# Turning back the second S5 half on GpSimd, with the S5 output products inside the inverse, in a two-layer hybrid decoder trunk

## The reference, cut to what matters

```
bu = einsum(u, b_bar);  states = scan: s[t] = lam_bar * s[t-1] + bu[t]      (complex, 1024 states)
y  = einsum(c_mat, states).real + d_skip * u;  y = gelu(y);  y = y * sigmoid(y @ glu_w + glu_b)
p  = softmax(q k^T / 8, causal);  y_moba = p @ v
g  = -exp(a_log) * softplus(a + dt_bias);  beta = sigmoid(b)
chunks of 64 tokens: (I + strictly_lower(beta k k^T * decay))^-1 applied to v and k, then a scan over 4 chunks
```

## Time and profile before

| | before |
|---|---|
| median of 3 runs | 1687.88 us (1685.31 to 1690.2) |
| the profiled execution, its own time | 1689.82 us |
| its span, first to last instruction | 1688.0 us |
| mean granted TensorE clock | 0.966 |
| TensorE busy | 1571.5 us, 93% of the span |
| VectorE busy | 1273.0 us, 75% |
| ScalarE busy | 920.9 us, 55% |
| GpSimd busy | 162.8 us, 10% |

### The profile page before, as it was taken

The page is one execution under the profiler, slowest core; times in us unless marked ns, Lnnn a source line. Parts: engine busy times, 40 slices in busy tenths (PEclk is TensorE's granted clock), DMA queues, the critical chain, the costliest instruction groups (busy, mean ns, idle before and its releaser), DMA issues.

```text
span 1688.0 us, 22489 instructions
## 1 busy us (share of the span) xinstructions
PE 1571.5 (93%) x8642; PEld 1267.0 (75%) x8642; DVE 1273.0 (75%) x1136; ACT 920.9 (55%) x761; POOL 162.8 (10%) x177
## 2 busy tenths in 40 slices
PE   8888999999898797599999999999999999999991
PEld 7657478888776574488888888888888888888881
DVE  7985655444529756388888888888888888888883
ACT  1144133434204331377777777777777777777770
POOL 0342085000004400200000000000000000000000
PEclk9989999999999998799999999999999999999996
DMA  8693165554433202699999999999999999999962
GB/s 311 247 314 137 52 218 205 198 176 152 171 133 118 76 3 100 237 363 374 355 395 391 355 394 370 375 395 348 398 394 349 395 395 350 396 389 366 393 254 89
DMA packets 192882, 469.57 MB, mean 278 GB/s; under 512 B 7024, under 2 KB 11248, under 8 KB 192304
## 3 DMA queue, kind: packets, MB, share of 16 engines
q1 hardware_dynamic: 189360, 453.70, 73.3%
q0 software_dynamic: 2304, 10.77, 1.6%
q10 hardware_dynamic: 1152, 4.19, 0.6%
HBM read 461.29 MB, written 25.17 MB: 288 GB/s over the span
## 4 chain that ended last, share of the span: by engine, by line
issue 59%; PE 28%; DVE 10%; DMA 1%; ACT 1%; POOL 1%; POOLq 0%; SPq 0%; DVEq 0%
PE ps L1429 9%; PE ps L1402 4%; PE ps L1440 4%; PE ps L1755 2%; DVE arena L960 2%; PE ps L1409 1%; PE ps L1693 1%; DVE arena L993 1%; PE ps L1707 1%; PE ps L1703 1%; DVE arena L977 1%; DVE small L1013 1%; DMA arena<-in_w_in 0%; DVE x L1021 0%; DVE x L1025 0%
## 5 line engine op out<-in xcount | busy, mean ns | idle before, releaser
L1036 DVE TENSOR_TENSOR lo<-arena,hi 128x2048 fp32r<-128x2048 f32 x378 | 868.4, 2302 | 222.5 <-ACT hi L641 221.9
L641 ACT ACTIVATE hi<-arena 128x2048 fp32r<-128x2048 f32 x378 | 723.3, 1919 | 356.8 <-PE ps L1429 229.8
L1429 PE MATMUL ps<-hi,xg 128*128 128x512 f32 x1792 | 556.0, 392 | 3.2 <-DVE xg L1042 2.6
L1429 PEld LDWEIGHTS ps<-hi,xg 128*128 128x128 f32 x1792 | 336.7, 189 | 75.9 <-DVE lo L1036 3.4
L1429 PE MATMUL ps<-lo,xg 128*128 128x512 f32 x896 | 350.1, 391 | 0.0
L1440 PE MATMUL ps<-hi,hTe 128*128 128x512 f32 x896 | 283.8, 398 | 2.2 <-DVE hTe L1066 2.2
L1429 PEld LDWEIGHTS ps<-lo,xg 128*128 128x128 f32 x896 | 169.0, 189 | 35.5
L1440 PEld LDWEIGHTS ps<-hi,hTe 128*128 128x128 f32 x896 | 164.8, 189 | 35.0 <-DVE lo L1036 2.6
L1440 PE MATMUL ps<-lo,hTe 128*128 128x512 f32 x448 | 175.8, 392 | 0.0
L1429 PE MATMUL ps<-hi,xs 128*128 128x512 f32 x448 | 140.1, 394 | 2.9 <-issue 2.9
L1402 PE MATMUL ps<-arena 128*128 128x256 f32 x544 | 126.2, 395 | 3.4 <-DMA arena<-in_w_in 2.2
(11 more groups left out here) (329 smaller groups left out, 1371.5 us busy)
## 6 DMA issues: line engine op xcount, KB each, us to landing
arena<-in_mg SPq DMA_DIRECT2D x112, 1024.0 KB, 7.0
arena<-in_mu SPq DMA_DIRECT2D x112, 1024.0 KB, 6.9
arena<-in_md SPq DMA_DIRECT2D x112, 1024.0 KB, 7.0
arena<-in_w_in SPq DMA_DIRECT2D x7, 2048.0 KB, 11.2
arena<-in_wg SPq DMA_DIRECT2D x14, 1024.0 KB, 5.1
arena<-in_wu SPq DMA_DIRECT2D x14, 1024.0 KB, 5.1
arena<-in_wd SPq DMA_DIRECT2D x14, 1024.0 KB, 4.9
xg_rows<-in_zeros SPq DMA_DIRECT2D x1, 8704.0 KB, 35.2
```

The lines of the kernel that those rows point to most:

```text
L641: af(hi[r % PARTS][:, :], raw[r % RAWS], ACT.Copy).then_inc(hi_ready, 1)
L1036: tt(lo[r % PARTS][:, :], raw[r % RAWS], hi[r % PARTS][:, :].bitcast(F32), ALU.subtract)\
L1429: ins = mm(ps[:, (4 if w == "G" else 4 + nb) + b, :], tok[a][:, kk * nt + b * P:kk * nt + (b + 1) * P], tiles_of(part[r % PARTS], w)[:, k, ...
```

## The change

Six edits:

1. `turn_forward(..., 1)` leaves VectorE. GpSimd runs it behind its whole convolution, once `turned_back` reaches its second count, and signals `states_ready`.
2. On VectorE, `convolve(l, 4)` now stands ahead of `s5_rotate(l, 1)`.
3. The norm of the probabilities moves behind the gates (behind the two `beta` operations).
4. TensorE's S5 output products move from ahead of L1626 to round `v == 2` of the inverse, behind its X and Y products, and write bank 7. VectorE's skip term moves to round `v == 3`, behind `kd` and the clearing of `S`.
5. The buffers move: `pT` to the start of `phase` (the cosine table), `M[0]` into the convolution's input, `uT`, `dt_`, `Tm`, `M[1]` and `tg` elsewhere.
6. New waits follow from that: ScalarE waits for `states_ready` before its first copy to `pT`, VectorE for `conv_v` before its first `M[0]`. TensorE no longer waits for `y_sum` between the transposes.

```diff
-O_PT = 8448
-O_LA, O_U, O_DT, O_T, O_A, O_MM = 0, 1536, 2304, 3072, 4608, 6144
-O_SQ, O_RN, O_TG = 512, 2816, 7680
+O_LA, O_U, O_DT, O_T, O_A, O_MM = 0, 1536, 2816, 3584, 4608, 7680
+O_SQ, O_RN, O_TG = 512, 2816, 512
...
-O_UT, O_QKM, O_MV, O_CIN, O_GW = 3072, 3584, 5120, 5888, 8736
+O_UT, O_QKM, O_MV, O_CIN, O_GW = 8224, 3584, 5120, 5888, 8736
+O_M0 = 6144
...
-        pT = zs(O_PT, 2304).rearrange("p (h n) -> p h n", h=NH)
+        pT = phase[:, 0:2304].rearrange("p (h n) -> p h n", h=NH)
-        M = [by_pair(O_MM), by_pair(O_MM + 1536)]
+        M = [zf(O_M0, 12 * CH).rearrange("p (i c) -> p i c", i=12), by_pair(O_MM)]
@@ gpsimd
-                pool.wait_ge(turned_back, l + 1)
+                pool.wait_ge(turned_back, 2 * l + 1)
                 pool.wait_ge(phase_ready, l + 1)
                 turn_forward(pool, step, 0).then_inc(turned, 1)
...
+                pool.wait_ge(turned_back, 2 * l + 2)
+                turn_forward(pool, step, 1).then_inc(states_ready, 1)
                 pool.wait_ge(pt_psum, NH * (l + 1))
@@ scalar
                 for h in range(NH):
                     act.wait_ge(pt_psum, NH * l + h + 1)
+                    if h == 0:
+                        act.wait_ge(states_ready, l + 1)
                     af(pT[:, h, :], ps[:, (2, 5)[h % 2], 0:384], ACT.Copy).then_inc(pt_evac, 1)
@@ vector, s5_recur
-                        if (jj, k, t) == (3, 1, 0):
+                        if (jj, k) == (3, 1):
                             ins.then_inc(turned_back, 1)
-                if t:
-                    step.wait()
-                    turn_forward(v_, step, 1).then_inc(states_ready, 1)
-                    dve.wait_ge(states_ready, l + 1)
@@ vector
                 convolve(l, 2)
+                convolve(l, 4)
                 s5_rotate(l, 1)
-                convolve(l, 4)
                 s5_recur(l, 1)
...
-                dve.wait_ge(sc_exp, 2 * NH * (l + 1))
-                step.then(v_.reciprocal(rinv, rsum))
-                for b, (c0, n) in enumerate(((0, P), (P, T))):
-                    tt(sc[...], sc[...], rinv[...], ALU.mult).then_inc(sc_norm, 1)
...
                 step.then(v_.reciprocal(beta, beta))
-                dve.wait_ge(y_psum, l + 1)
-                (the two operations of the skip term, from bank 5)
+                (the norm of the probabilities, as it stood above)
...
+                    if g == 0:
+                        dve.wait_ge(conv_v, l + 1)
                     tt(M[0][:, ij, :], LA[:, ij, 1, :], ...)
@@ vector, round v == 3
                         v_.memset(S, 0.0).then_inc(s_zero, 1)
+                        dve.wait_ge(y_psum, l + 1)
+                        (the two operations of the skip term, from bank 7)
@@ tensor
-                (waits for c_ready, turned, states_ready, proj_evac; the 32 matmuls of the S5 output into bank 5)
...
-                    if h == 1:
-                        pe.wait_ge(y_sum, l + 1)
@@ tensor, behind round v's X and Y products
+                    if v == 2:
+                        pe.wait_ge(c_ready, l + 1)
+                        pe.wait_ge(turned, l + 1)
+                        pe.wait_ge(states_ready, l + 1)
+                        pe.wait_ge(kv_evac, 3 * (l + 1))
+                        (the 32 matmuls of the S5 output into bank 7)
```

More of the change, by code:

```diff
@@ L1131, in _ @@
                 stt(l1, xx, -1.0, xx, ALU.mult, ALU.max).then_inc(gate_in, 1)
-                dve.wait_ge(sc_exp, 2 * NH * (l + 1))
-                step.then(v_.reciprocal(rinv, rsum))
-                for b, (c0, n) in enumerate(((0, P), (P, T))):
-                    tt(sc[:, :, c0:c0 + n], sc[:, :, c0:c0 + n],
-                       rinv[:, 6 * b:6 * b + 6].unsqueeze(2).to_broadcast([P, NH, n]), ALU.mult)\
-                        .then_inc(sc_norm, 1)
                 dve.wait_ge(gate_ln, 2 * (l + 1))
@@ L1150, in _ @@
                 step.then(v_.reciprocal(beta, beta))
-                dve.wait_ge(y_psum, l + 1)
[L1153 to L1159, removed]
+                dve.wait_ge(sc_exp, 2 * NH * (l + 1))
+                step.then(v_.reciprocal(rinv, rsum))
+                for b, (c0, n) in enumerate(((0, P), (P, T))):
+                    tt(sc[:, :, c0:c0 + n], sc[:, :, c0:c0 + n],
+                       rinv[:, 6 * b:6 * b + 6].unsqueeze(2).to_broadcast([P, NH, n]), ALU.mult)\
+                        .then_inc(sc_norm, 1)
                 dve.wait_ge(gs_evac, l + 1)
@@ L1221, in _ @@
                         v_.memset(S, 0.0).then_inc(s_zero, 1)
+                        dve.wait_ge(y_psum, l + 1)
+                        for f in range(2):
+                            stt_out = stt(ys[:, f, :], uT[:, f, :], par[:, PO["d"] + 2 * l + f:PO["d"] + 2 * l + f + 1],
+                                          ps[:, 7, f * T:(f + 1) * T], ALU.mult, ALU.add)
+                            if f:
+                                stt_out.then_inc(y_sum, 1)
+                            else:
+                                step.then(stt_out)
                 for b in range(NB):
@@ L1604, in _ @@
                 features(2, 0, w[5], 0).then_inc(proj_psum, 1)
[L1606 to L1615, removed]
                 pe.wait_ge(qk_ready, l + 1)
@@ L1719, in _ @@
                                 ins.then_inc(kv_psum, 1)
+                    if v == 2:
[3 more added lines that the diff above has]
+                        pe.wait_ge(kv_evac, 3 * (l + 1))
+                        for f in range(2):
+                            for r in range(2):
+                                for q in range(4):
+                                    ins = mm(ps[32 * q:32 * q + 32, 7, f * T:(f + 1) * T], c_mat[:, 4 * f + q, r, :],
+                                             states[r][:, 4 * f + q, :], start=(r == 0), stop=(r == 1))
+                        ins.then_inc(y_psum, 1)
                 pe.wait_ge(xy_used, 15 * (l + 1))
```

## The result

The changed kernel is slower: 1705.01 us in the median (1704.1 to 1706.92) against 1686.9 (1685.31 to 1690.2), ratio 1.0106 with a 95% interval of 1.0088 to 1.0125, that is 18 us (15 to 21). The profiled execution took 1704.81 us; its span is 1703.0 us at a mean clock of 0.962, where before it was 1688.0 at 0.966.

A forecast was written before the change was run, and what follows sets the result against it. Bounds: the chain up to the first copy into pT, and the inverse's rounds, set by TensorE. Layer 0: 3.4 + 2.5 - 0.2 + 1.8 + 0.9 = 8.4; layer 1: 7.8; together 16.2 over 1687.9, so 1704 (1693 to 1713).

The forecast's parts named there:

- The gates: VectorE's chain up to the gate sums: g_ready near 112.8 in layer 0, 7 us earlier than 120.00; decays end near 118.
- GpSimd's queue: Tile 8 (6.0 us), then the turn (14.3 plus 2.6), end at 132.1; first copy to pT 3.4 and 2.8 us later.
- The port: SBUF port during GpSimd's turn: one two-input VectorE operation per turn operation; GpSimd loses about VectorE's operation less 0.35, 2.6 us.
- The clock: TensorE, idle some 9 us, runs from first pT copy to first A product at 1.2 GHz: 2.5 us per layer (0 to 4.5).
- rival 2: VectorE becomes last: an M[0] and the U fall behind the value products, 3 to 5 us more per layer, near 1712; chance 0.2.
- The S5 output: Inverse, per layer: 32 products in round 2 cost 1.8 us; skip term ahead of round 3's last subtractions costs 0.9.
- The sum: Whole kernel: 8.4 us more in layer 0 and 7.8 in layer 1, together 16.2, so 1704 against the median of 1687.9.
- Rival 3: GpSimd's turn done before TensorE's decays, before about 125 in layer 0: 4 us gained per layer, 1680; chance 0.04.

The follow-up runs named there:

- turn_first: Changed kernel with GpSimd's turn of the second half ahead of its tile 8 instead of behind; ratio 1.0058, 10 us over the kernel before.
- kept_busy_longer: Changed kernel with 20 further, unused 128x384 matmuls behind TensorE's decays, so that it works until ScalarE's first copy to pT; ratio 1.0073.
- vector_turn: Changed kernel with the turn of the second half alone back on VectorE; ratio 1.0029, 5 us over the kernel before.
- order_only: Kernel before with edits 2 and 3 alone: third convolution ahead of the rotation, norm of the probabilities behind the gates; ratio 0.9989.
- norm_only: Kernel before with edit 3 alone: norm of the probabilities behind the gates; ratio 0.9975.
- split_turn: Changed kernel with the second half's turn shared, VectorE real part, GpSimd imaginary; pT off the table, skip term behind the last subtractions; ratio 0.9995.
- split_early_decay: split_hidden with VectorE's ekl directly behind beta, ahead of the norm of the probabilities; ratio 0.9952, 8 us under the kernel before.
- kept_busy: Changed kernel with 16 further, unused 128x384 matmuls behind TensorE's decays; ratio 1.0088.
- pt_elsewhere: Changed kernel with pT in free space instead of on the cosine table, so ScalarE's copies wait for no turn; ratio 1.0047, 8 us over the kernel before.
- split_hidden: split_turn with the S5 output products ahead of the turning of M[0] and the skip term ahead of the first X and Y products; ratio 0.9968.

## Why the prediction was right

The forecast was 1704 (1693 to 1713), slower with 0.90. Measured: 1705.0. By its steps:

- **The gates.** `g_ready` 7 us early; the table says 8.4 and 8.8. That TensorE would follow k's products directly and keep its clock through the decays was wrong: it idled 1.99 us ahead of the gate sums, and the clock is 0.72 from 114 to 120. The decays ended at 120.1, which is 118.6 when the later start of 1.5 us is taken off, near the 118 forecast, because the sums had begun earlier. This error cost nothing, since GpSimd was later still.
- **GpSimd's queue.** Tile 8 was put at 6.0 us and took 6.5 (110.52 to 117.03), the turn at 16.9 and took 16.6. The first copy was to be 3.4 and 2.8 us later than before. It was 3.5 and 3.0, released by L550 in both layers. Within the turn the parts moved against each other. The terms listed for VectorE's disturbance add up to 2.8 us and not to the 2.6 given, and 2.3 were measured. Only the second operation of the norm fell into the turn, where L545 took 3.87 us; the first fell beside tile 8. The tiny `ekl`, which the count of six operations left out, took 2.32 and stood in the place that this left.
- **The port.** One VectorE operation with two SBUF inputs for each turn operation, as said. The Trainium skill (SBUF — State Buffer, "Who interferes with whom") has whoever starts first keep the port for its whole instruction, and the trace agrees for VectorE: `ekl` on 128x12 starts at 118.60 and ends at 120.92, just as GpSimd's L545 does (120.90). It agrees for GpSimd too, which the prediction read otherwise. In the earlier trace rows VectorE's operation (L1036, 3.15 us from 252.63) ended at 255.78, 2.07 us after GpSimd's start at 253.71, and GpSimd lost 1.94; L545 lost 1.5 us (3.87 against 2.35), and the norm beside it ended 1.65 us after its start. What GpSimd waits for is the rest of VectorE's operation, and not its length less 0.35. In turn_first a `COPY` and a `TENSOR_SCALAR` of 128x12, with one SBUF input, also took 2.21 and 2.32 us, while the `TENSOR_TENSOR` with two behind the latter, started at 112.37 as GpSimd went from one turn operation to the next (112.39), took 0.16. The same section names copy and tensor_scalar among the operations that can take both ports, under conditions on their operands, which agrees.
- **The clock.** Put at 2.5 us less 0.2, measured 2.8 and 3.1, and shown by kept_busy_longer, not only argued. TensorE's idle time ahead of it was put at 9 us and was 12.9, since its two transposes were done at 120.8 (119.3 without the later start) and not at 123; the price of the clock did not hang on that. The deeper waits that had also seemed possible for this stretch (rival 2) are out: VectorE waited 8.91 us for TensorE there, after its first `U`.
- **The S5 output.** Put at 1.8 and 0.9, measured 1.9 to 2.0 and 0.6.
- **The sum.** 8.4 and 7.8 us per layer forecast, 8.2 and 8.6 in the profiles. The mechanism and the size of each term held. That the total comes within 1 us is in part luck: the clock was put too low and the skip term too high, and layer 0's round 0 became 0.7 us shorter (6.12 against 6.82 us from its first A product to the next round's), 0.46 of it a stop of TensorE that the changed kernel does not have (last section).

Rival 3's threshold was put at 125 in layer 0. turn_first ended the turn at 124.9 and was still slower than before. That rival priced only GpSimd's end and left out what an early turn does to the small gate operations: the same port that delays `M[0]` then stands on the gates' path. What I had not seen at all is that edit 2 costs VectorE 2.3 us ahead of its scans. In the changed kernel this is hidden behind GpSimd; it shows in vector_turn's gate sums, which come 1.1 and 1.4 us later than before although the norm has left their path, and in order_only against norm_only.

How much of GpSimd's lateness would remain if it had its six operations but no port were shared, was not tried: no run here takes the port away from it.

## What to carry to other kernels

Work that goes from a busy engine to an idle one is paid at the idle one's rate and in its queue's order: ask when that queue can start it, what else stands behind it, and whether a buffer that it still reads has been given to someone else. When TensorE waits longer than before, look at the granted clock of what follows: here half clock made 7.8 us into 10.6 and 10.9. When VectorE and GpSimd both work from SBUF, count VectorE's operations, however small, and not only their time: here each cost up to a whole operation of GpSimd's, and one of them three. An operation in a stretch that one engine fills completely had its full price here even though it was free where it stood before.

## What the runs showed of the hardware that was not expected

In layer 0's rounds, some runs see TensorE stop while no engine or DMA that the profile names holds it. The chain of turn_first:

```profile
139.84 0.68 PE ps L1682 x16
...
143.32 2.66 issue
145.98 1.90 PE ps L1705 x12
```

It is 0.46 us in the kernel before, 1.38 in vector_turn, 2.66 in turn_first and 2.71 in split_turn. norm_only has two (0.61 and 0.87), order_only three (0.33, 0.60, 0.43), split_early_decay one of 0.62, kept_busy and kept_busy_longer one of some 0.4. The changed kernel, pt_elsewhere and split_hidden have none above 0.3 in these rounds, so reaching the rounds early does not decide it. In turn_first the large DMAs of the start are still running:

```profile
141.00:143.00 2.00, 2.00 (x76) 2.00 (x73) 1.38 (x4) 0.00 (x0) 1.42 (x1) 1.00 1.05 386
143.00:145.00 2.00, 0.32 (x11) 0.18 (x7) 1.15 (x3) 0.00 (x0) 0.00 (x0) 1.00 0.95 347
145.00:147.00 2.00, 1.02 (x9) 1.05 (x10) 0.00 (x0) 0.00 (x0) 0.00 (x0) 0.99 0.25 96
...
146.00:150.00 4.00, 4.00 (x52) 3.67 (x54) 0.00 (x0) 0.55 (x2) 0.00 (x0) 0.62 0.02 8
```

There the stop ends as the DMA traffic does, from a share of 0.95 to 0.25. In split_turn it does not: the stop lasts from 139.35 to 142.06, and the share is still 1.01 from 142 to 144. The last line shows the second cost of such a stop, a clock of 0.62 in the 4 us behind it.

The transfers of the DMA queue q8, whose kind the profile calls "instruction", fit every case. They are of 16 KB and take 0.9 to 1.5 us, and in the rounds, where TensorE is the one engine with hundreds of instructions, they come about 4 us apart. In turn_first one runs from 143.43 to 144.52, inside the stop, and TensorE goes on at 145.98; the one before it had started at 127.60. In split_turn it is 139.55 to 140.67, and TensorE goes on at 142.06. In all twelve stops named above TensorE goes on 1.2 to 1.5 us after such a transfer has ended. So TensorE seems to wait for its next instructions there. This is read from traces alone: the profile does not say for which engine a transfer is, what made some of them late (the large DMAs beside them, or what stands ahead in a queue) is open, and no run tested it. In layer 1, with little DMA traffic, no such stop is longer than 0.3 us.
